# Prompt block 1 runs ahead of the other prompt blocks, and its experts run inside their mixers

## The reference, cut to what matters

```
h = rmsnorm(x); z = h @ w_in                       # 5888 columns, for mixer A, mixer B, gates
oa = sliding-window attention (8 heads, chunks of 64, window 128)
ob = retention (4 heads, a state carried from chunk to chunk), normed, times silu(rg)
x1 = x + (sigmoid(ga) * (oa @ wa) + sigmoid(gb) * (ob @ wb)) @ w_out
h2 = rmsnorm(x1); q = h2 @ w_q; top 16 keys of 128 on two sides, 8 heads -> 128 experts of 16384 a token
y = rmsnorm(x1 + sum over the 128 experts of gate * gelu(h2 . u[expert]) * v[expert])
```

## Time and profile before

| | us |
|---|---|
| median of 3 timed runs | 4421.74 (4421.59 to 4427.8) |
| the profiled execution's own time | 4377.7 |
| its span | 4376.1 |
| first projection, 0 to 107.9 | 107.9 |
| sample mixer, to 276.9 | 169.0 |
| big projection with the sample experts, to 991.7 | 714.8 |
| prompt mixers with the copy, to 1610.2 | 618.5 |
| prompt experts, to the end | 2765.9 |

### The profile page before, as it was taken

How to read it: one execution, slowest core, us unless ns; L and a number is a source line. 1 busy time by engine, 2 the same in 40 slices (tenths; PEclk the granted TensorE clock), 3 DMA queues, 4 the chain that set the end, 5 groups by cost and what they waited for, 6 DMA issues and landing times.

```text
span 4376.1 us, 34385 instructions
## 1 busy us (share of the span) xinstructions
PE 3523.6 (81%) x9469; PEld 1729.9 (40%) x9469; DVE 2341.1 (53%) x4875; ACT 1132.8 (26%) x3155; POOL 1700.3 (39%) x1567
## 2 busy tenths in 40 slices
PE   7659999995888846987987987987887887777776
PEld 4425666664554523432332332332332332222222
DVE  0214777503434315675675675675675675675444
ACT  2101111112222111333332332332332333332322
POOL 0000766301222210445445455445445445455554
PEclk9679999996888967999999999999999999999999
DMA  6461999719799981999999999999999999999998
GB/s 271 141 240 48 412 414 413 304 42 343 261 317 294 313 287 68 377 421 421 407 421 421 402 422 421 405 417 421 398 421 422 403 420 421 417 415 420 419 421 356
DMA packets 279813, 1537.89 MB, mean 351 GB/s; under 512 B 28528, under 2 KB 58224, under 8 KB 140016
## 3 DMA queue, kind: packets, MB, share of 16 engines
q0 software_dynamic: 225072, 1356.43, 77.6%
q1 hardware_dynamic: 37968, 155.97, 9.2%
q10 hardware_dynamic: 16640, 24.12, 1.5%
HBM read 1493.29 MB, written 178.52 MB: 382 GB/s over the span
## 4 chain that ended last, share of the span: by engine, by line
DMA 30%; PE 18%; issue 7%; DVE 2%; ACT 2%; POOL 1%; ACTq 0%; POOLq 0%; DVEq 0%
DMA ring<-uv_d,IXD_p 30%; PE ps L1244 15%; PE ps L1214 3%; DVE ring L1445 2%; ACT dg L1294 1%; POOL ring L1562 1%; ACT GE_p L1288 1%; DVE BV_p L680 0%; DVE DOT_p L1445 0%; ACTq L1293 0%; PE ps L1207 0%; PE ps L1229 0%; POOLq L1558 0%; PE ps L1221 0%; DVE X L1436 0%
## 5 line engine op out<-in xcount | busy, mean ns | idle before, releaser
L1244 PE MATMUL ps<-ring,dg 128*128 128x512 f32 x4096 | 1944.0, 611 | 515.3 <-ACT dg L1294 511.6
L1562 POOL DMA_INDIRECT ring<-uv_d,IXD_p x1024 | 1276.7, 1247 | 1480.3 <-PE ps L1244 1163.3
L1445 DVE CUSTOM_DVE_ANT_0 ring<-ring,H 128x1024 f32<-128x1024 f32 x1024 | 1250.4, 1223 | 998.4 <-DMA ring<-uv_d,IXD_p 978.4
L1244 PEld LDWEIGHTS ps<-ring,dg 128*128 128x128 f32 x4096 | 744.6, 192 | 1569.4 <-ACT dg L1294 818.3
L889 PE MATMUL ps<-w,xg 128*128 128x368 f32 x2048 | 635.0, 473 | 2.3 <-ACT SC_s L639 2.3
L1288 ACT ACTIVATE GE_p<-DOT_p 128x2 f32<-128x2 f32 x512 | 104.1, 203 | 1680.0 <-DVE DOT_p L1445 1680.0
L889 PEld LDWEIGHTS ps<-w,xg 128*128 128x128 f32 x2048 | 389.8, 190 | 247.0 <-issue 3.8
L1294 ACT ACTIVATE dg<-gdi,GE_p 128x128 f32<-128x128 f32 x1024 | 355.1, 394 | 65.7 <-issue 8.5
L1282 ACT ACTIVATE gdi<-ident,GD_p 128x128 f32<-128x128 f32 x1024 | 346.5, 386 | 19.7 <-issue 19.5
L1214 PE MATMUL ps<-wq,hT_p 128*128 128x512 f32 x512 | 256.6, 603 | 39.4 <-ACT hT_p L1252 39.4
L670 POOL DMA_INDIRECT ring_s<-in_peer_u,IXD_s x128 | 136.5, 1067 | 214.0 <-DVE IXD_s L769 161.0
(11 more groups left out here) (284 smaller groups left out, 2316.7 us busy)
## 6 DMA issues: line engine op xcount, KB each, us to landing
uv_d<-in_peer_u POOLq DMA_DIRECT2D x128, 512.0 KB, 17.7
uv_d<-in_peer_v POOLq DMA_DIRECT2D x128, 512.0 KB, 18.8
w<-in_w_in SPq DMA_DIRECT2D x8, 2944.0 KB, 10.8
w<-in_w_in SPq DMA_DIRECT2D x16, 1472.0 KB, 9.5
z_d<-zo ACTq DMA_DIRECT2D x16, 1472.0 KB, 20.0
ring<-uv_d,IXD_p POOLq DMA_INDIRECT x1024, 11.2
gates<-z_d SPq DMA_DIRECT2D x8, 1536.0 KB, 11.8
mixers<-z_d SPq DMA_DIRECT2D x8, 1408.0 KB, 15.9
```

The costliest lines, as they stand in the source:

```text
L1244: mm = T.matmul(bank(6 + n), dg[:, k % DR, :], ring[:, k % RS, D + n * 512:D + (n + 1) * 512], start=(k == 0), stop=(k == NK - 1))
L1445: V.tensor_tensor_reduce(out=row, in0=row, in1=H2[:], scale=1.0, scalar=0.0, op0=ALU.mult, op1=ALU.add, accum_out=DOT[:, k:k + 1]).then_in ...
L1562: g.indirect_dma_start(ring[:, n % RS, :], None, uv_d, bass.IndirectOffsetOnAxis(ap=IXD[:, n:n + 1], axis=0)).then_inc(s_ring[n % RS], 16)
```

## The change

Block 1 no longer goes with the other prompt blocks.

- The first projection makes z of blocks 0 and 1 (32 groups in place of 16); z of block 1 is kept in `Z1` and stored to `z_d` in four parts.
- The sample mixer's SP now loads x and stores x1 and h2, behind the state stores. POOL copies pieces 0 to 43 of the tables, once `wb` is in.
- The big projection makes the keys of blocks 0 and 1, then z of blocks 2 to 8 (16 tiles of 7 groups). The scores of block 1 have a buffer of their own, and DVE searches block 1 between the sample experts' tiles and leaves places and gates in `IXD1` and `GD1`. POOL first copies pieces 88 to 127, then gathers for the sample experts. The gelus stand at n = 16, 28, ..., 100, the exponentials at 12 and 70. Loops are written out.
- A new stage holds the mixers of block 1 alone, gated half included, while POOL copies pieces 44 to 87 once all branch weights are in.
- The stage of the later mixers handles blocks 2 to 8. It loads its tables and weights anew. z comes in three parts (`zqk`, `zv` double, `gates`); x1, h2 and x go over SP; `HO` lies over `yT`. At six points of `dve_block` (seven in the last block) DVE takes three tiles of block 1's u rows (dots), and from block 3 on three tiles of v rows (values) of six groups before. `ru` and `rv` have three buffers each. ScalarE takes a gelu over 18 columns after each block. The rest of the values, the final norm and y of block 1 stand around the last gated half.
- The expert stage starts at block 2 (`FB`), with seven blocks in place of eight.

The core of the diff:

```diff
-TABLE_PER = NEXP // P // (NB - 1)
+EARLY = 1
+TABLE_BS, TABLE_E, TABLE_CS = 44, 88, 128
...
                     for n in range(WT):
-                        act.wait_ge(s_mm, n + 1)
-                        S.activation(Z[:, n * WC:(n + 1) * WC], ps[:, n % AB, 0:WC], ACT.Copy, scale=rstd[:, 0:1]).then_inc(s_zact, 1)
+                        for b in range(2):
+                            m = 2 * n + b
+                            act.wait_ge(s_mm, m + 1)
+                            S.activation((Z1 if b else Z)[:, n * WC:(n + 1) * WC], ps[:, m % AB, 0:WC], ACT.Copy, scale=rstd[:, b:b + 1]).then_inc(s_zact, 1)
...
-        def pool_table(g, blk):
-
-            with g.Fori(0, TABLE_PER) as i:
-                part = (blk - 1) * TABLE_PER + i
+        def pool_table(g, lo, hi):
+
+            with g.Fori(lo, hi) as part:
                 g.dma_start(uv_d[bass.ds(part * P, P), 0:D], rows(t["peer_u"], part)).then_inc(s_uv, 16)
                 g.dma_start(uv_d[bass.ds(part * P, P), D:], rows(t["peer_v"], part)).then_inc(s_uv, 16)
...
# sample mixer, GpSimd
-                    load_rows(g, 0)
-                    store_block(g, 0)
-                    g.wait_ge(s["x1st"], 16)
-                    g.wait_ge(s["h2st"], 16)
+                    g.wait_ge(s_wb, 16)
+                    g.sem_inc(s_pool, 1)
+                    pool_table(g, 0, TABLE_BS)
...
# mixers of block 1 alone, GpSimd
+                    g.wait_ge(s_wb, 16 * 5)
+                    g.sem_inc(s_pool, 1)
+                    pool_table(g, TABLE_BS, TABLE_E)
...
# big projection, GpSimd
+                    g.wait_ge(s_cw, 16 * (KT + 3))
+                    g.sem_inc(d["pool"], 1)
+                    for p in range(2):
+                        g.wait_ge(s_w[p], 16 * (WT // 4) + 16)
+                        g.sem_inc(d["pool"], 1)
+                    pool_table(g, TABLE_E, TABLE_CS)
+                    g.wait_ge(c["v1"], 3)
+                    g.sem_inc(d["pool"], 1)
                     pool_gathers(g, 0)
...
# big projection, ScalarE
+                        if n == GATES1_AT:
+                            act_gates(act, 1)
+                        if gelu_at(n) is not None:
+                            act_gelu(act, 0, gelu_at(n))
...
# later mixers
+        PG = 3
+        SET = 6 * PG
+        SETS = NK // SET
...
+            def dve_expert_dots(v, grp):
+                for k in places(grp):
+                    row = ru[:, k % PG, :]
+                    v.wait_ge(s_ring[8 + k % PG], BASE_R + 16 * (k // PG + 1))
+                    V.tensor_tensor_reduce(out=row, in0=row, in1=H21[:], scale=1.0, scalar=0.0, op0=ALU.mult,
+                                           op1=ALU.add, accum_out=DOT1[:, k:k + 1]).then_inc(d["freed"], 1)
...
+            def dve_point(v, blk, j):
+
+                grp = 6 * (blk - 2) + j
+                if blk > 2 and j < 6:
+                    dve_expert_values(v, grp - 6)
+                dve_expert_dots(v, grp)
...
+            def pool_values(g, grp):
+                if grp:
+                    g.wait_ge(d["accz"], BASE_V + grp * PG)
+                    g.sem_inc(d["pool"], 1)
+                for k in places(grp):
+                    g.indirect_dma_start(rv[:, k % PG, :], None, t["peer_v"],
+                                         bass.IndirectOffsetOnAxis(ap=IXD1[:, k:k + 1], axis=0)).then_inc(s_ring[11 + k % PG], 16)
+
+            def pool_dots(g, grp):
+                if grp:
+                    g.wait_ge(d["freed"], BASE_U + grp * PG)
+                    g.sem_inc(d["pool"], 1)
+                for k in places(grp):
+                    g.indirect_dma_start(ru[:, k % PG, :], None, t["peer_u"],
+                                         bass.IndirectOffsetOnAxis(ap=IXD1[:, k:k + 1], axis=0)).then_inc(s_ring[8 + k % PG], 16)
...
+                    for blk in range(2, NB):
+                        for j in range(7 if blk == NB - 1 else 6):
+                            grp = 6 * (blk - 2) + j
+                            if blk > 2 and j < 6:
+                                pool_values(g, grp - 6)
+                            pool_dots(g, grp)
...
+                    for blk in range(2, NB):
+                        act_block(act, blk, blk % 2, blk > 2)
+                        act_set(act, blk - 2)
...
# tail of the later mixers, VectorE
                     dve_gate(v, NB - 1)
+                    for grp in range(LAST - 6, LAST - 3):
+                        dve_expert_values(v, grp)
                     dve_merge(v, NB - 1)
+                    for grp in range(LAST - 3, LAST + 1):
+                        dve_expert_values(v, grp)
                     dve_residual(v, NB - 1)
...
# prompt experts
-                    with g.Fori(1, NB) as blk:
+                    with g.Fori(FB, NB) as blk:
```

More of the change, by code:

```diff
@@ new lines, in trunk_kernel, with z, load_keys_part, load_values_part @@
+        HALF = {0: "z1", 1: "z1b"}
+        def z(lo, n, half=0):
+            if lo < VB:
+                return zqk[:, lo:lo + n]
+            return zv[:, half, lo - VB:lo - VB + n] if lo < RG else gates[:, lo - RG:lo - RG + n]
+        def load_keys_part(sp, blk):
+            sp.dma_start(zqk[:], rows(z_d[:, 0:VB], blk)).then_inc(s["zq"], 16)
+        def load_values_part(sp, blk):
+            sp.dma_start(zv[:, blk % 2], rows(z_d[:, VB:RG], blk)).then_inc(s[HALF[blk % 2]], 16)
+        def wait_mixers(eng, blk, half):
+            eng.wait_ge(s["zq"], 16 * blk)
+            eng.wait_ge(s[HALF[half]], 8 * (blk - half) + 16)
@@ L896, in _ @@
                     act.sem_inc(s_zact, AB)
[L897 to L898 removed]
+                    for blk in range(2):
+                        act_keys_first(act, blk)
+                        act_keys_second(act, blk)
                     for n in range(WT * PB):
@@ new lines, in trunk_kernel @@
+            (zqk, zv, gates, X, Pr, qbT, kbT, atm, oaT, yn, yT, bg, gf, wa, wb, wo, qaT, qdT, alibi, intra, into,
+             outd, kdec, sink, mx, ngm, es, rs, stats, mv, sdv, sm2) = prompt_buffers(b_, "_p")
+            PT, HO = over(Pr, yT)
+            ru = sb(b_, "ru", [P, PG, D])
+            rv = sb(b_, "rv", [P, PG, D])
+            AC1 = sb(b_, "AC1", [P, D])
+            H21 = sb(b_, "H21", [P, D])
+            DOT1, GE1, WG1 = [sb(b_, n, [P, NK]) for n in ("DOT1", "GE1", "WG1")]
+            m41 = sb(b_, "m41", [P, 4])
@@ new lines, in dve_expert_values @@
+            def dve_expert_values(v, grp):
+                if grp % 6 == 0 and grp // 6 < SETS:
+                    cols = set_columns(grp // 6)
+                    v.wait_ge(d["gelu"], BASE_G + grp // 6 + 1)
+                    V.tensor_tensor(WG1[:, cols], GE1[:, cols], GD1[:, cols], ALU.mult).then_inc(d["wgt"], 1)
+                    v.wait_ge(d["wgt"], BASE_W + grp // 6 + 1)
+                for k in places(grp):
+                    row = rv[:, k % PG, :]
+                    v.wait_ge(s_ring[11 + k % PG], BASE_R + 16 * (k // PG + 1))
+                    if k == 0:
+                        V.tensor_scalar(AC1[:], row, WG1[:, k:k + 1], None, ALU.mult).then_inc(d["accz"], 1)
+                    else:
+                        v.wait_ge(d["accz"], BASE_V + k)
+                        V.scalar_tensor_tensor(AC1[:], row, WG1[:, k:k + 1], AC1[:], ALU.mult, ALU.add).then_inc(d["accz"], 1)
@@ L1086, in _ @@
+                    load_values_part(sp, 2)
+                    load_tables(sp)
+                    sp.dma_start(H21[:], rows(h2_d, 1)).then_inc(s_h2, 16)
+                    load_gates(sp, 2)
+                    load_rows(sp, 2)
+                    load_branches(sp)
                     for src, dst in ((KA, o["kp"]), (VA, o["vp"])):
                         sp.dma_start(dst, z_d[(NB - 1) * P:, src:src + P]).then_inc(s_copy, 16)
-                    load_mixers(sp, 2, 0)
-                    with sp.Fori(1, NB // 2) as pair:
-                        for half in range(2):
-                            blk = 2 * pair + half
+                    for blk in range(2, NB):
+                        if blk + 1 < NB:
+                            sp.wait_ge(s["stn"], blk)
+                            load_values_part(sp, blk + 1)
+                            sp.wait_ge(s["qkv"], 2 * blk + 2)
+                            sp.wait_ge(s["kdec"], blk)
+                            load_keys_part(sp, blk + 1)
+                        if blk > 2:
@@ L1141, in _ @@
                 def _(act):
-                    act_block(act, 1, 1, False)
-                    with act.Fori(1, NB // 2) as pair:
-                        for half in range(2):
-                            act_block(act, 2 * pair + half, half, True)
-                    act_block(act, NB - 1, 0, True)
+                    for blk in range(2, NB):
+                        act_block(act, blk, blk % 2, blk > 2)
+                        act_set(act, blk - 2)
                     act_gate(act, NB - 1)
```

594 lines of the change are left out of this document (342 added, 252 removed).

## The result

The changed kernel took 4502.03 us (median of 4 runs, 4485.11 to 4504.98), the kernel before 4421.66 (4 runs, 4416.57 to 4427.8): a ratio of 1.0159, 95% interval 1.0119 to 1.0198. It is slower, by 80 us where 87 were forecast. The profiled execution is the shortest of its four, 4485.11 us with a span of 4483.6, so against the span of before (4376.1) the two traces differ by 107.5 us, and they are compared with each other. The trace of before is of an execution 39 us shorter than any of the four timed ones, so of those 107.5 us some 27 are no part of the timed difference.

A forecast was written before the change was run, and what follows sets the result against it. The bound was taken to change by stage, with the expert stage DMA-bound. Terms +75 + 12 - 7 + 336.5 - 329.5 = +87 gave 4465 against 4377.7, or 4509 against the median 4421.7; forecast's own range 4450 to 4570.

The forecast's parts named there:

- Expert stage: Last stage, prompt experts: one block of eight leaves it, prologue and ends stay; -329.5 us.
- First projection: Opening stage: gains block 1's 16 groups (+79.4), loses weight waits (-8.8), larger load and last store some 4; +75 us.
- Sample mixer: Sample mixer stage: 44 copy pieces slow the output weight's load, and two last stores queue behind state stores; +12 us.
- Block 1 alone, and the wait behind it: Block 1's mixer stage and after: copy outlasts it by 78 us, holding block 2's first dots until 235 us after its start.
- Big projection: Big projection stage: loses 16 groups (-79.4), gains block 1's search keys (42), leftover copy (+25), gelu wait (+5); -7 us.
- the gelu's place: Big projection: ScalarE's first gelu, fixed ahead of eviction 16, waits for gathered rows; hidden by 4 us only, taken as +5.
- The mixers with experts: Later mixers: 70.0 us a block becomes 92 with block 1's dots and values on DVE, which is then the bound.
- the bubble: Later mixers: with three buffers a side, DVE waits for gathers at two pairs of back-to-back points; +7.2 us a block.
- The copy does not hold the gathers: Rival, block 2's first dots: copy drains before DVE asks, so they come 97 us earlier; 4412 us, chance 8%.
- Hidden in idle time: Rival, later mixers: block 1's experts vanish in DVE's idle time, 76 us a block, -96; 4413 us, chance 8%.
- TensorE's clock: Rival, later mixers: branch products run at the lower clock, 46 us instead of 23, +17 a block; 4611 us, chance 8%.

The follow-up runs named there:

- the first experiment: Changed kernel with the 44 copy pieces of block 1's own mixer stage moved to the head of the big projection; 4535.07 us, ratio to before 1.025.
- The fastest version: Changed kernel with copy boundaries 30, 45, 85, block 1's expert groups placed apart, and each gather waiting for its own buffer alone; 4244.88 us, ratio to before 0.9712.

## Why the prediction was right, and where it was not

The sum was right to 7 us of the timed difference, with one step wrong and one term near only because its errors offset. Against the traces: +71.0 first projection, +44.1 sample mixer, +204.0 block 1's stage, -0.2 big projection, +117.2 later mixers, -328.6 expert stage, together +107.5. That is 20 us over the forecast, with errors of +32 and -15 in it that offset each other in part; that the timed difference lies only 7 us away is in part luck, since the terms were worked out from a trace shorter than the timed executions.

- **Expert stage**, -329.5 forecast, -328.6 measured. **First projection**, +75 and +71.0. Both terms hold.
- **Sample mixer**, +12 forecast with +38 "if the stage's end waited for the copy itself". It did: +44.1. I had the right mechanism as a bound and chose against it. That the next stage would give most of it back did not come true either.
- **Block 1 alone, and the wait behind it** is the step that failed. It said that 44 pieces outlast the stage, that the gathers of block 1's experts queue behind them, and that VectorE waits 60 to 110 us at the first dots of block 2. The stage's own length was right (119 with its stores; 115.2 without copies), and so was the size of the overhang (78; 88.8 measured between the changed kernel and the first experiment). Its place was not: the closing barrier takes it, before the next stage may begin. And the big projection, not block 2, is next, so by the time of block 2's dots nothing of any copy is left. The total still fits: from the start of block 1's mixer to the first dots the traces have 204.0 + 23.0 = 227 us (leaving out the projection between) where 235 were forecast, and 713 from there to the stage's end where 720 were; 321.2 in place of 336.5. "Whether POOL blocks on issues and so closes the first stage later changes little" made the number come out right: the wait is paid once, wherever it stands. It matters for the remedy. A wait at the first dots would call for another order of GpSimd's queue; a wait at the barrier calls for another stage, and that one edit, 44 pieces to the later mixers, was worth 74 us.
- **Big projection**, -7 forecast, -0.2 measured, and near only by luck. The +25 for copy left over from the stage before did not come, since the barrier had already waited for that copy: the keys start 25.6 us into the stage, as before (25.2), and take 43 more (42 forecast). First dots came 187 us into the stage (782.90), not 230, so the gelu's place held nothing, and the 40 pieces hid behind TensorE (the run with them behind the gathers). That alone would make about -36. In their place the products took 36 us more than 112 groups of before's length: 23.4 in gaps inside groups, the rest in products that ran longer; see the last section. The fastest version, with the same code there and no such gaps, took 679.4, which is -35.4.
- **The mixers with experts**, 92 us a block forecast, 92.4 measured (1453.31 to 1915.43, five blocks). The parts hold roughly: VectorE busy 71.5 us, 4.2 for the exponentials, 2.5 for the gate's Silu, and the bubbles at two places a block. Only the bubble was mis-sized, 7.2 forecast, 9.8 to 13.7 of gather waits in three blocks (9.8 in the one shown), and I had read it as the DMA's round trip alone; 59 us of the stage went with the wait for a whole group. VectorE's share is 69 to 79%, not over 80, and TensorE's 60 to 68%.
- **Rivals.** "The copy does not hold the gathers" was true and did not make the kernel faster: its price of -97 left out that the barrier would wait. "Hidden in idle time" (76 a block) was not reached even by the best version, 81.2. "TensorE's clock" fell out: in a block TensorE's branch products took 9.6 and 13.9 us (9.1 and 13.9 before), and VectorE waited 0.6 us for them over the stage:

```profile
1603.22 9.62 PE L305 MATMUL ps<-wa_p,oaT_p 128*128 128x512 f32 x16 [2.83 <-DVE atm_p L676]
1612.68 13.90 PE L308 MATMUL ps<-wb_p,yT_p 128*128 128x512 f32 x32
```

The granted clock of the later mixers did fall, from 0.83 to 0.74. The Trainium skill, "TensorE: Matmul & The Clock Gate", section "HAM oscillation", says that idle gaps bring it down; the trace agrees in the mean, but the branch products ran at 1.00 from 1612 on.

What the change does for the time, then: taking a block out of the DMA-bound stage gave 328.6 us. The first projection took back 71.0, block 1's own mixers 115.2 without copies, and the later mixers, a block fewer but with block 1's experts inside, 117.2, together 303.4. It lost because 88 pieces of copy were put into two short closed stages with room for about 45, and because gathers waited for whole groups. Both can be undone with the change kept, and then it is 2.9% faster than before.

## What to carry to other kernels

A copy issued from GpSimd that nothing in its stage needs still had to land before a closed stage ended; no run tried one from another queue. Count each stage's room, its own time less what its transfers take, and put no more pieces in it: in block 1's stage (15) and at the projection's head (40) pieces below the room were free, above it one cost 2.4 to 3.2 us in the three stages tried. Spread over the later mixers the same pieces cost 0.5 to 1.1. A stage with a long DMA tail behind idle engines shows as a window in which every engine reads 0.00 and DMA does not. In a ring of buffers let each load wait for its own buffer only, and before a piece of VectorE work is moved ahead of another, ask which wait the other one was covering.

## What the runs showed of the hardware

- With 84 pieces at the projection's head GpSimd issued 57 of them in some 90 us and then stopped at an issue for 119.4 us; with 44 pieces or fewer it never stopped. The Trainium skill, "DMA: Bandwidth & Descriptors", section "SWDGE vs HWDGE vs iDMA", says that GpSimd appends its descriptors to rings that the engines drain. Whether a full ring is what stopped it is not shown: no run here varied the piece's size.
- In the projection TensorE paused inside single groups of eight products, where it waits for no semaphore. In the changed kernel the pauses begin near 851 us, at a granted clock of 1.00 (780 to 850), and the clock stands at 0.50 from 855 to 880. Its timeline:

```profile
861.89 0.77 PE L1137 MATMUL ps<-w,xg 128*128 128x368 f32 x1 [0.66 <-issue]
864.69 0.77 PE L1137 MATMUL ps<-w,xg 128*128 128x368 f32 x1 [2.03 <-issue]
```

It lasts some 28 us, with DMA's share at 1.03, against 1.02 in the 70 us ahead of it, in which TensorE was busy for 69.8. Such idle time, 7.8 to 30.9 us, is in every trace of the first three sets of runs with the new structure, in neither of the last set (whose projection took 676 and 679 us), and not in the trace of the kernel before, whose DMA was as full for 300 us. That trace (4377.7 us) is as short as the fourth set's executions of the same kernel, so whether the longer executions of before have such pauses isn't known. No run was made on it; its cause stays open.
- The same kernel before took 4421.66, 4425.88 and 4423.21 us in three sets of runs and 4371.83 in the fourth, 1.1% less, so only ratios within a set are compared.
